# Queries' low parts and the second copy of the keys' high parts written by VectorE into the other 64 partitions, in place of small DMAs

## The reference

```python
h = rms_norm(x, g_pre); proj = h @ w_in           # 1024 -> 7424 columns, split into eleven parts
q = partial_rope(b_q)                             # 8 query heads of 64
k, v = partial_rope(b_k), b_v                     # 2 key/value heads of 64, 4 query heads to each
scores = einsum(q block of 128, k of 3 blocks) / 8, masked to |q - k| <= 128
p = softmax over the 384 keys and one sink logit per head
yb = (p @ v) * silu(b_z)
```

## Time and profile before

| | us |
|---|---|
| runs, median of 3 | 1049.53 |
| all runs | 1049.53, 3597.86, 1049.29 |
| profiled execution, first to last instruction (span) | 1047.3 |
| TensorE busy in it | 1021.4 |
| VectorE busy in it | 471.7 |
| ScalarE busy in it | 338.2 |
| GpSimd busy in it | 166.9 |

### The profile page before, as it was taken

How to read it: one execution, slowest core, us unless ns; L and a number is a source line. 1 busy time by engine, 2 the same in 40 slices (tenths; PEclk the granted TensorE clock), 3 DMA queues, 4 the chain that set the end, 5 groups by cost and what they waited for, 6 DMA issues and landing times.

```text
span 1047.3 us, 13011 instructions
## 1 busy us (share of the span) xinstructions
PE 1021.4 (98%) x4716; PEld 835.7 (80%) x4716; DVE 471.7 (45%) x890; ACT 338.2 (32%) x551; POOL 166.9 (16%) x85
## 2 busy tenths in 40 slices
PE   4999999999999999999999999999999999999997
PEld 3888888888777777777888878888888888887886
DVE  5524322334476676665357343443344322126434
ACT  6321221222355454444221243343332212115121
POOL 1112221212011111100221002111121212120000
PEclk9999999999999999999999999999999999999999
DMA  5312111111011111110212231100110111160322
GB/s 219 103 50 54 59 40 60 40 61 48 31 49 49 48 48 48 38 28 21 81 40 101 81 101 45 43 32 30 50 61 30 31 60 50 40 248 2 103 98 81
DMA packets 21339, 65.41 MB, mean 62 GB/s; under 512 B 3232, under 2 KB 4384, under 8 KB 21056
## 3 DMA queue, kind: packets, MB, share of 16 engines
q1 hardware_dynamic: 20992, 64.39, 18.6%
q10 hardware_dynamic: 320, 0.66, 0.4%
HBM read 56.51 MB, written 4.19 MB: 58 GB/s over the span
## 4 chain that ended last, share of the span: by engine, by line
PE 93%; DVE 4%; ACT 1%; DMA 1%; issue 0%; SPq 0%; DVEq 0%; ACTq 0%
PE pm L377 24%; PE pm L379 24%; PE pm L378 24%; PE pv L481 3%; PE pm L618 3%; PE pm L620 3%; PE pm L619 3%; PE sa L460 2%; PE sa L467 2%; PE sa L459 2%; PE pv L590 1%; PE pm L542 1%; PE sa L574 1%; DMA area_m<-in_x 1%; DVE area_m L914 1%; PE sa L581 1%
## 5 line engine op out<-in xcount | busy, mean ns | idle before, releaser
L377 PE MATMUL pm<-h_hi,units_r 128*128 128x512 f32 x928 | 364.6, 393 | 3.5 <-DVE h_lo L928 3.2
L379 PE MATMUL pm<-h_hi,units_r 128*128 128x512 f32 x928 | 361.9, 390 | 0.0
L378 PE MATMUL pm<-h_lo,units_r 128*128 128x512 f32 x928 | 361.8, 390 | 0.0
L340 POOL TENSOR_TENSOR units_r<-units,units_r 128x1024 fp32r<-128x1024 f32 x80 | 165.7, 2071 | 761.0 <-ACT units_r L639 761.0
L377 PEld LDWEIGHTS pm<-h_hi,units_r 128*128 128x128 f32 x928 | 174.8, 188 | 39.8 <-DVE h_lo L928 4.0
L379 PEld LDWEIGHTS pm<-h_hi,units_r 128*128 128x128 f32 x928 | 174.6, 188 | 36.5
L378 PEld LDWEIGHTS pm<-h_lo,units_r 128*128 128x128 f32 x928 | 174.9, 188 | 35.1
L639 ACT ACTIVATE units_r<-units 128x1024 fp32r<-128x1024 f32 x90 | 91.6, 1018 | 198.8 <-PE pm L379 172.3
L1168 DVE TENSOR_TENSOR area_a<-area_a,pm 128x1024 f32<-128x1024 f32 x15 | 18.3, 1222 | 139.5 <-PE pm L379 139.5
L377 PE MATMUL pm<-y_hi,units_r 128*128 128x512 f32 x192 | 76.9, 400 | 0.0
L379 PE MATMUL pm<-y_hi,units_r 128*128 128x512 f32 x192 | 75.0, 390 | 0.0
(11 more groups left out here) (153 smaller groups left out, 1031.6 us busy)
## 6 DMA issues: line engine op xcount, KB each, us to landing
units<-in_w SPq DMA_DIRECT2D x58, 512.0 KB, 3.3
units<-in_wup SPq DMA_DIRECT2D x24, 256.0 KB, 2.6
area_m<-in_x SPq DMA_DIRECT2D x8, 512.0 KB, 7.6
units<-in_wmem SPq DMA_DIRECT2D x8, 512.0 KB, 3.3
area_a<-in_wout SPq DMA_DIRECT2D x2, 2048.0 KB, 9.9
units<-in_x SPq DMA_DIRECT2D x8, 512.0 KB, 3.9
out<-area_a SPq DMA_DIRECT2D x7, 512.0 KB, 2.9
area_a_r<-area_m SPq DMA_DIRECT2D x16, 128.0 KB, 2.3
```

What stands on the lines that cost most here:

```text
L340: nc.gpsimd.tensor_tensor(w_lo[:, p, 0:width], raw[:, p, 0:width], w_hi[:, p, 0:width].bitcast(F32), ALU.subtract).then_inc(lo_made, 1)
L377: pe.matmul(pm[:, p, cols], hi, src_hi[:, k, cols], start=(k == 0), stop=False)
L378: pe.matmul(pm[:, p, cols], hi, src_lo[:, k, cols], start=False, stop=False)
L379: mm = pe.matmul(pm[:, p, cols], lo, src_hi[:, k, cols], start=False, stop=(k == chunks - 1))
```

## The change

VectorE writes the low queries straight into the other half of `q_stack`, and copies the high keys twice, once into each half of `k_hi`. The four DMAs per block, the buffer `q_low` and the semaphore `qk_moved` are gone. TensorE's `scores` waits for `qk_staged`, and SyncE loads weights in one plain loop.

```diff
--- before.py
+++ after.py
@@ -150,7 +150,6 @@
 
         q_stack = area_r[:, QZ0:QZ0 + 2 * GROUP * P].rearrange("p (g h q) -> p g h q", g=2, h=GROUP)
         q_stack_f32 = q_stack.bitcast(F32)
-        q_low = area_m[:, QL0:QL0 + GROUP * P].rearrange("p (h q) -> p h q", h=GROUP)
 
         k_hi = area_mr[:, KWH0:KWH0 + 2 * WIN].rearrange("p (g k) -> p g k", g=2)
         k_lo = area_r[:, KWL0:KWL0 + WIN]
@@ -215,7 +214,6 @@
         swapped, roped = sem("swapped"), sem("roped")
         v_turned, v_made = sem("v_turned"), sem("v_made")
         sig_made, y_made, y_hi_made, y_ready = sem("sig_made"), sem("y_made"), sem("y_hi_made"), sem("y_ready")
-        qk_moved = sem("qk_moved")
         qk_staged, v_staged = sem("qk_staged"), sem("v_staged")
         scored, masked, nm_ready, exped = sem("scored"), sem("masked"), sem("nm_ready"), sem("exped")
         p_ready, turned, pt_hi_made, pt_lo_made = sem("p_ready"), sem("turned"), sem("pt_hi_made"), sem("pt_lo_made")
@@ -262,22 +260,8 @@
                 sp.wait_ge(lo_made, 2 * i + t0)
                 sp.dma_start(raw[:, 1, 0:AW], wup[i + up0]).then_inc(raw_landed[1], 16)
 
-            def move_qk(i):
-
-                sp.wait_ge(qk_staged, i + 1)
-                for g in range(2):
-                    own, other = slice(g * HEAD, (g + 1) * HEAD), slice((1 - g) * HEAD, (2 - g) * HEAD)
-                    sp.dma_start(q_stack_f32[other, g, :, :], q_low[own, :, :]).then_inc(qk_moved, 16)
-                    sp.dma_start(k_hi[other, g, :].bitcast(F32), k_hi[own, g, :].bitcast(F32)).then_inc(qk_moved, 16)
-
-
-            move_qk(0)
-            for i in range(2):
+            with sp.Fori(0, KC) as i:
                 merge_loads(sp, i, T_MA, T_MA, 0)
-            with sp.Fori(2, KC) as i:
-                move_qk(i - 1)
-                merge_loads(sp, i, T_MA, T_MA, 0)
-            move_qk(NB - 1)
             n8 = T_MA + KC
             sp.wait_ge(lo_made, T_ZB - 1)
             sp.dma_start(raw[:, 0, :], w8[n8]).then_inc(raw_landed[0], 16)
@@ -444,7 +428,7 @@
             def scores(i, g):
 
                 if g == 0:
-                    pe.wait_ge(qk_moved, 64 * i + 64)
+                    pe.wait_ge(qk_staged, i + 1)
                 own = slice(g * HEAD, (g + 1) * HEAD)
                 for h in range(GROUP):
                     b = BANKS[h % 3]
@@ -985,14 +969,14 @@
 
             def stage_qk(i, at, window):
 
-                await_count(dve, qk_moved, 64 * i)
                 own = [slice(g * HEAD, (g + 1) * HEAD) for g in range(2)]
                 for g in range(2):
                     nc.vector.tensor_copy(q_stack[own[g], g, :, :], qT[own[g], :, at])
+                    nc.vector.tensor_copy(k_hi[own[1 - g], g, :], kT[own[g], window])
                     ins = nc.vector.tensor_copy(k_hi[own[g], g, :], kT[own[g], window])
                 link(ins)
                 for g in range(2):
-                    nc.vector.tensor_tensor(q_low[own[g], :, :], qT[own[g], :, at],
+                    nc.vector.tensor_tensor(q_stack[own[1 - g], g, :, :], qT[own[g], :, at],
                                             q_stack_f32[own[g], g, :, :], ALU.subtract)
                     ins = nc.vector.tensor_tensor(k_lo[own[g], :], kT[own[g], window],
                                                   k_hi[own[g], g, :].bitcast(F32), ALU.subtract)
```

## The result

The changed kernel takes 1054.18 us (median of 5 runs, 1051.77 to 1054.99), the one before 1049.29 beside it (five runs, 1047.36 to 1049.53 but for the disturbed one). The ratio is 1.0049, 95% interval 1.0036 to 1.0062: slower by half a per cent. The forecast was 1050.5 with a range up to 1053.5, so it was too low. The profiled execution is the one of 1054.18 us.

The account below looks back on a forecast made before the run. TensorE was taken to bound the kernel. Transfers 0, block 0 +1.01 and other blocks 0 gave about +1.0 us, a span of 1048.3; with runs some 2.2 above the span, 1050.5 us, range 1049.0 to 1053.5.

Parts of the forecast that it names:

- The bound and the places: TensorE bounds the kernel; in the attention stage only block 0 was to lengthen it, by 1.01 us.
- the removed transfers: Attention stage: taking away the sixteen query and sixteen key transfers gains 0, as no TensorE wait hangs on them.
- the second transposes of block 0: Where TensorE waits for VectorE's scalings: its gap was to grow from 0.43 to 1.44 us.
- their longer staging: Blocks 1 to 6: the 1.01 us is covered; in block 1, 2.05 us are free.
- The first stagings met GpSimd out of sight: Around 239.71, block 0's own staging: delayed subtractions meet GpSimd's split, hidden by idle time behind it.
- The length: VectorE's staging inside block 0 grows by 1.01 us, with bounds of 0.54 and 1.4.
- The rule behind it: VectorE staging: an instruction whose written half changes waits out its predecessor; 1.01 us with it, 0.54 to 0.70 without.
- the decisive 0.90: Block 0: past 0.90 us of added staging, the fourth scaling starts after GpSimd's split at 295.47.
- The step that failed: Block 0's fourth scaling: VectorE keeps the access, GpSimd waits 0.5 us unfelt, and the forecast, chance 0.39, stands.
- The rival: Block 0: GpSimd slips between the scalings, TensorE waits 3.4 us later than before, 1052.9 us; chance 0.28.
- the rule of the first to issue: VectorE's two-port modes and GpSimd exclude each other for a whole instruction; would put GpSimd's 295.47 ahead of 295.58.
- the base of 1049.5: Starting time of the whole kernel: runs of 1049.29 and 1049.53, some 2.2 us above the profiled span.

Follow-up runs that it names:

- e1: Kernel before, with VectorE writing the low queries into the other half and the key copies still going by DMA; ratio 1.0006.
- e3: Kernel before, all DMAs kept, with two more 64x384 key copies (own half, unused memory) in block 0's staging; ratio 1.0003.
- e9: Kernel before, all DMAs kept, with three more 64x384 key copies (own half, unused memory) in block 0's staging; ratio 1.0013.
- e2: Kernel before, with VectorE making the second key copy and the low queries still going by DMA; ratio 1.0040.
- e4: Kernel before, all DMAs kept, with four more 64x384 key copies (own half, unused memory) in block 0's staging; ratio 1.0058.
- e5: Changed kernel, with ScalarE's high part that releases GpSimd's split made later in block 0 alone; ratio 1.0005.
- e6: Kernel of e5 with four further 64x384 copies (own half, unused memory) in block 0's staging; ratio 1.0031.
- e7: Kernel of e5 with eight further 64x384 copies (own half, unused memory) in block 0's staging; ratio 1.0054.
- e8: Changed kernel without staging keys again where the window stays the same (blocks 1 and 7); 1047.53 us, ratio 0.9995.
- e10: Kernel before, DMAs kept, without staging keys again or their transfers where the window stays the same (blocks 1 and 7); ratio 0.9999.
- e11: Changed kernel of e8 with block 0's value staging also moved ahead of the last gating of the convolution; 1047.53 us, ratio 0.9996.

## Why the prediction was wrong, step by step

**The bound and the places were right.** Nothing came of the removed transfers; the second transposes of block 0 are where the time goes; blocks 1 to 6 cover their longer staging. The first stagings met GpSimd out of sight at 239.84, as foretold, and both sides show in the rows: GpSimd's split took 2.89 us instead of 2.39 behind the third subtraction, and the fourth then took 2.66 instead of 0.55:

```profile
240.49 2.66 DVE L981 TENSOR_TENSOR area_a_r<-area_a,area_m_r 64x384 fp32r<-64x384 f32 x1
```

**The length was mis-sized a little.** Taken 1.01, measured 1.13: a held instruction starts 0.02 us after its predecessor's end, not at it. The rule behind it, that the written half counts alone, was right (e1). The error doesn't matter, since both values lie past the decisive 0.90. That a longer staging costs its length up to there held to 0.01 us: 0.54 and 0.81 us of copies lengthened the gap by 0.53 and 0.81 (e3, e9).

**The step that failed** is the choice inside the fourth scaling's meeting with GpSimd: "If VectorE's row of instructions keeps the access, GpSimd waits 0.5 us, which nobody feels, and the forecast stands." It doesn't keep it. e2, e4 and the changed kernel have the fourth scaling caught whenever its start comes after GpSimd's, by 0.05 us, by 0.18 or by 0.23. The rival had this at 3.4 us, measured 3.2, and at 1052.9 for the whole. I had written down the rule of the first to issue, which favoured the rival, and still gave it the smaller chance.

**A term was missing** in the forecast and in every rival: behind the gap of 3.64 us TensorE ran some 3 us at the lower clock, 1.4 to 1.5 us lost; the gaps of 2.65 to 3.72 us in the experiments did the same, those of 0.43 to 1.56 us did not. The trace could have warned. At the start of the kernel before, TensorE waits 2.38 us for VectorE, one of the waits for line 928 in the earlier trace rows, and the granted clock falls behind it:

```profile
27.20 0.50 PE L377 MATMUL pm<-h_hi,units_r 128*128 128x512 f32 x1 [2.38 <-DVE h_lo L928]
```

```profile
25.00:30.00 5.00, 2.80 (x10) 2.36 (x11) 4.27 (x7) 2.18 (x3) 3.32 (x2) 0.79 0.79 269
30.00:35.00 5.00, 5.00 (x28) 4.23 (x27) 2.73 (x4) 2.27 (x4) 0.00 (x0) 0.86 0.48 151
```

With this term and the measured 3.2 the rival would have read 1050.5 - 1.0 + 3.2 + 1.5 = 1054.2. That it is the measured median to a tenth is luck: the base of 1049.5 comes from two runs, and with the two further ones of the kernel before, 1047.36 and 1048.27, their median is 1048.8.

## What to carry to other kernels

Where an engine off the bound is just ahead of the bounding one, price an added piece of work against two clocks: the slack before the reader needs it, and the start of the next instruction of another engine that excludes it. Past the second, a tenth of a microsecond can cost microseconds: a staging 0.81 us longer cost 0.74 in the stretch (e9), one 0.95 us longer 5.85 (e2). A gap in the bounding engine can cost more than its length, when the granted clock falls with it. Of a long chain of equal blocks look at the first and the last by themselves; here the first had no slack, and did work that was not needed.

## What was not expected

The same wait does not always lower the clock. All thirteen profiled executions have the wait for this line between 24 and 28 us, 2.33 to 2.38 us long. In eight (before, after, e1, e3, e4, e5, e6, e9) the granted clock falls behind it; in five (e2, e7, e8, e10, e11) it stays up. The kernel before has the rows just above, that of e8:

```profile
25.00:30.00 5.00, 3.07 (x18) 2.55 (x19) 4.60 (x6) 2.43 (x4) 3.05 (x2) 1.00 0.81 288
30.00:35.00 5.00, 5.00 (x34) 4.32 (x33) 3.27 (x5) 2.94 (x5) 0.00 (x0) 1.00 0.40 135
```

So the length of a gap alone does not decide between 1.56 us, where the clock stayed up, and 2.65, where it fell, each in one profiled execution. What else decides was not tried.

The runs of one kernel differ accordingly. Of the 29 runs of the kernel before beside the last experiments, the 17 with a mean granted clock of 0.999 have a span of 1045.34 us on the mean, the 9 with 0.997 have 1046.96. These 1.6 us are larger than the effects of e1, e3, e5 and e9 and blur them in the runs; the stretch between two fixed events, taken behind that start, shows them to about 0.15 us. The changed kernel's quickest run, 1051.77, has a mean clock of 0.997 against 0.993 to 0.995 for the others, so one of the two falls, at the start or in block 0, is likely missing in it. It was not profiled, and which one it was is not known.
